# Both pairs of down-projection blocks of a gated conv-FFN by seven products, evicted by ScalarE and summed by accumulating DMAs

## What is computed

```python
def rms_norm(x, g):
    xf = x.astype(jnp.float32)
    return (xf * lax.rsqrt(jnp.mean(xf * xf, axis=-1, keepdims=True) + EPS)) * g

def conv_gated_ffn(x, w_up, conv_w, conv_b, w_down):     # x 256 x 2048, w_up 2048 x 11264
    gu = x @ w_up
    gate, up = gu[..., :D_FF], gu[..., D_FF:]            # D_FF = 5632
    gate = causal_depthwise_conv(gate, conv_w, conv_b)   # three taps along the tokens
    return (jax.nn.silu(gate) * up) @ w_down             # w_down 5632 x 2048

h = h + conv_gated_ffn(rms_norm(h, norm_ffn_g[i]), w_up[i], conv_w[i], conv_b[i], w_down[i])
```

## Time and profile before

| | |
|---|---|
| median of 3 runs | 2156.36 us (2156.32 to 2156.4) |
| profiled execution | 2156.12 us, span of its instructions 2154.3 us |
| PE busy | 2141.7 us (99%), 11526 matmuls |
| PE weight load busy | 1859.3 us (86%) |
| DVE busy | 1707.6 us (79%) |
| ACT busy | 1125.1 us (52%) |
| POOL busy | 50.4 us (2%) |
| DMA | 406.75 MB, mean 189 GB/s, the load queue 55.0% of 16 engines |

### The profile page before, as it was taken

The page is one execution under the profiler, slowest core; times in us unless marked ns, Lnnn a source line. Parts: engine busy times, 40 slices in busy tenths (PEclk is TensorE's granted clock), DMA queues, the critical chain, the costliest instruction groups (busy, mean ns, idle before and its releaser), DMA issues.

```text
span 2154.3 us, 32719 instructions
## 1 busy us (share of the span) xinstructions
PE 2141.7 (99%) x11526; PEld 1859.3 (86%) x11526; DVE 1707.6 (79%) x2192; ACT 1125.1 (52%) x1422; POOL 50.4 (2%) x114
## 2 busy tenths in 40 slices
PE   9999999999999999999999999999999999999998
PEld 8898888888888888888898988888888888888886
DVE  5797569888889888897557875788888889888964
ACT  6556445554555544555554664445544545544554
POOL 2000000000000000000000000000000000000011
PEclk9999999999999999999999999999999999999999
DMA  8645555546555546555556455555556555556562
GB/s 269 213 139 174 178 200 188 182 158 233 205 204 178 182 166 234 197 192 195 173 183 182 138 176 176 201 203 176 186 177 234 195 197 176 183 185 234 176 216 97
DMA packets 233323, 406.75 MB, mean 189 GB/s; under 512 B 14828, under 2 KB 50268, under 8 KB 233096
## 3 DMA queue, kind: packets, MB, share of 16 engines
q1 hardware_dynamic: 231976, 402.72, 55.0%
q0 software_dynamic: 512, 1.76, 0.2%
q10 hardware_dynamic: 736, 1.07, 0.1%
HBM read 403.42 MB, written 2.10 MB: 188 GB/s over the span
## 4 chain that ended last, share of the span: by engine, by line
PE 97%; ACT 1%; DVE 1%; issue 1%; POOL 0%; POOLq 0%; DVEq 0%; ACTq 0%
PE acc L2082 16%; PE tps L2082 16%; PE acc L1901 12%; PE acc L1903 12%; PE acc L1902 12%; PE tps L2092 9%; PE acc L2092 9%; PE tps L1902 3%; PE tps L1903 3%; PE tps L1901 3%; PE acc L1988 1%; PE tps L1958 1%; ACT sq_h L773 0%; DVE h L1536 0%; DVE xb_lo L1193 0%
## 5 line engine op out<-in xcount | busy, mean ns | idle before, releaser
L996 ACT ACTIVATE w_hi<-raw 128x1024 fp32r<-128x1024 f32 x540 | 559.2, 1058 | 536.3 <-PE acc L2092 116.6
L1566 DVE TENSOR_TENSOR w_lo<-raw,w_hi 128x1024 fp32r<-128x1024 f32 x540 | 650.2, 1225 | 161.5 <-ACT w_hi L996 149.8
L1181 DVE TENSOR_TENSOR w_lo<-raw,w_hi 128x1024 fp32r<-128x1024 f32 (+1 forms) x288 | 342.0, 1211 | 143.2 <-ACT w_hi L722 137.6
L722 ACT ACTIVATE w_hi<-raw 128x1024 fp32r<-128x1024 f32 (+2 forms) x287 | 290.2, 1044 | 179.5 <-PE acc L1903 126.3
L2082 PE MATMUL acc<-xa,w_hi 128*128 128x512 f32 x1536 | 366.0, 391 | 0.0
L2082 PE MATMUL tps<-xa,w_hi 128*128 128x512 f32 x1536 | 361.2, 390 | 0.0
L2082 PEld LDWEIGHTS tps<-xa,w_hi 128*128 128x128 f32 x1536 | 285.3, 188 | 57.2
L2082 PEld LDWEIGHTS acc<-xa,w_hi 128*128 128x128 f32 x1536 | 283.7, 188 | 56.2 <-DVE h L1521 0.4
L1902 PE MATMUL acc<-w_hi,xb_lo 128*128 128x512 f32 x640 | 249.0, 389 | 0.0
L1901 PE MATMUL acc<-w_hi,xb_hi 128*128 128x512 f32 x560 | 220.5, 394 | 0.4 <-ACT pw L1072 0.4
L1903 PE MATMUL acc<-w_lo,xb_hi 128*128 128x512 f32 x560 | 218.1, 389 | 0.0
(11 more groups left out here) (262 smaller groups left out, 2651.1 us busy)
## 6 DMA issues: line engine op xcount, KB each, us to landing
raw<-in_w_up SPq DMA_DIRECT2D x176, 1024.0 KB, 5.0
raw<-in_w_down SPq DMA_DIRECT2D x88, 1024.0 KB, 5.0
raw<-in_w_out SPq DMA_DIRECT2D x32, 1024.0 KB, 5.0
raw<-in_w_ple_gate SPq DMA_DIRECT2D x32, 1024.0 KB, 5.1
raw<-in_w_in SPq DMA_DIRECT2D x21, 1024.0 KB, 5.4
raw<-in_w_ukv SPq DMA_DIRECT2D x8, 1024.0 KB, 5.5
raw<-in_w_in SPq DMA_DIRECT2D x8, 864.0 KB, 4.8
raw<-in_w_uq SPq DMA_DIRECT2D x6, 1024.0 KB, 5.7
```

The source lines that it names most:

```text
L722: copy(w_hi[:, half_of(m), 0:n], raw[:, c % RAW_SLOTS, at:at + n], ACT.Copy).then_inc(hi_done, 1)
L996: copy(w_hi[:, half_of(m), :], raw[:, c % RAW_SLOTS, half * HALF:(half + 1) * HALF], ACT.Copy).then_inc(hi_done, 1)
L1181: dve.tensor_tensor(w_lo[:, half_of(m), 0:n], raw[:, c % RAW_SLOTS, at:at + n], w_hi[:, half_of(m), 0:n].bitcast(F32), ALU.subtract).then_ ...
L1566: dve.tensor_tensor(w_lo[:, half_of(m), :], raw[:, slot, half * HALF:(half + 1) * HALF], w_hi[:, half_of(m), :].bitcast(F32), ALU.subtract ...
```

## The change

The down product of unit u - 1 is now seven products for both pairs of blocks (0 and 1: `second` = 0; 2 and 3: `second` = 1). A unit has 30 halves in two phases of 15: the gate's 8 halves with the first pair's seven products between them, then the up's 8 halves with the second pair's seven. Within a phase the x halves are at places 0, 1, 2, 3, 5, 8, 11, 14 (`X_AT`), the products B11, B21, B22, T1, T3, T2, T4 at 4, 6, 7, 9, 10, 12, 13 (`FORM_AT`). The loop turns over one unit, and the last unit stands behind it with its second phase "apart" (x halves first, then products). The products of phase A use `tps`, those of phase B `acc`. up_sum and gated of a unit move to the start of the next one.

DVE adds no product any more. ACT evicts each into a buffer `stage` in SBUF, scaled by token where it goes to `h` (`take`, 14 a unit), and POOL adds it with a DMA that accumulates from `stage` into `h` or a sum (`products_added`, 14 a unit, 256 KB each). TensorE waits on `staged` for banks; ACT waits on `stage_free`, which POOL raises when a phase's seven DMAs have landed. There are now two sets of four sums (`corner_b` is new), s_hi and s_lo have their own place, the last unit's low part goes from POOL to DVE, and ACT waits for `stage_free` before the squares of the ple part.

The core of the diff (declarations, the semaphores' count functions, and renamed arguments are left out):

```diff
+        X_AT = (0, 1, 2, 3, 5, 8, 11, 14)
+        FORM_AT = (4, 6, 7, 9, 10, 12, 13)
...
+
+            return max(n for n in range(UNIT_HALVES) if raw_half(n, apart)[0] == c)
+
...
+                def load_at(l, v, n, apart, pieces):
                     slot = (c + n) % RAW_SLOTS
-                    first = M_UNIT + i * UNIT_HALVES + 2 * RAW_SLOTS
                     if n < RAW_SLOTS:
-                        freed = max(LAST_LO[n] + 1 - UNIT_HALVES, 2 * (n + 1) - 2 * RAW_SLOTS)
+                        freed = max(last_lo(n + 2 * RAW_SLOTS, False) + 1 - UNIT_HALVES, 2 * (n + 1) - 2 * RAW_SLOTS)
                     else:
-                        freed = 2 * (n - RAW_SLOTS) + 2
...
+                def load_unit(l, u, v, apart):
+                    for second in range(2):
+                        last = apart and second == 1
+                        for k, n in enumerate(X_CHUNK_APART if last else X_MIXED):
+                            if n == (4 if last else 5):
+                                break
+                            load_at(l, v, PHASE_CHUNKS * second + n, apart,
+                                    (rows(w_up, l, 4 * k, 4, u * BLK + D_FF * second, BLK), CHUNK, BLK))
+                        for k, n in enumerate(Q_APART if last else Q_MIXED):
+                            load_at(l, v, PHASE_CHUNKS * second + n, apart,
+                                    (rows(w_down, l, v * 4, 4, (2 * second + k) * BLK, BLK), CHUNK, BLK))
+                        if not last:
+                            load_at(l, v, PHASE_CHUNKS * second + X_MIXED[3], apart,
...
+                def products_added(v, second):
+                    p1, p7, p6, p5 = sums[second]
+                    j = 2 * second
+                    for k, dst in ((B11, p1), (B21, h[:, 0, j * BLK:(j + 1) * BLK]),
+                                   (B22, h[:, 0, (j + 1) * BLK:(j + 2) * BLK]), (T1, p5), (T3, p7), (T2, p6),
+                                   (T4, h[:, 1, j * BLK:(j + 1) * BLK])):
+                        pool.wait_ge(staged, taken(l, v, second, k + 1))
+                        pool.sem_inc(stage_seen, 1)
+                        pool.dma_start(dst, stage[:, k, :], accum_op=ALU.add).then_inc(added, 16)
+                    pool.wait_ge(added, 16 * 7 * phases(l, v, second))
+                    pool.sem_inc(stage_free, 1)
...
+                    def take(second, k, bank, scale=None):
+                        n = PHASE * second + (FORM_APART if apart and second else FORM_AT)[k]
+                        halves_used(act, l, M_UNIT + n, v)
+                        if k == B11:
+                            act.wait_ge(stage_free, phases(l, v, second))
+                        if scale is not None:
+                            copy(stage[:, k, :], bank, ACT.Copy, scale=rstd["ffn"][:, scale:scale + 1]).then_inc(staged, 1)
+                            return
+                        copy(stage[:, k, :], bank, ACT.Copy).then_inc(staged, 1)
 
...
                     go(0, 2)
-                    halves_used(act, l, m0 - 1, w)
+                    up_low(u - 1, lambda: halves_used(act, l, M_UNIT - 1, v))
+                    go(2, 3)
                     act.wait_ge(g_done, UNITS * l + u)
...
-                    copy(s_hi.rearrange("p c k s -> p (c k s)"), up_f[:, :, :].rearrange("p a s -> p (a s)"),
+                    go(3, 5)
+                    act.wait_ge(s_step, 4 * (UNITS - 1) * l + 4 * v + 4)
+                    copy(s_hi[:, :, :, :].rearrange("p c k s -> p (c k s)"), up_f[:, :, :].rearrange("p a s -> p (a s)"),
                          ACT.Copy).then_inc(s_split_hi, 1)
...
+                    take(0, B11, tps[:, 0, :])
                     go(7, 9)
-                    for k in range(2):
...
-                first_unit(l)
-                with act.Fori(0, LOOPS) as w:
-                    for i in range(TURN_UNITS):
-                        unit(l, w, i)
-
-                act.wait_ge(g_done, UNITS * l + UNITS)
-                copy(xa[0][:, 0:4, :], conv[:, :, :], ACT.Copy).then_inc(g_hi, 1)
+                    take(0, B21, tps[:, 1, :], 0)
+                    go(9, 10)
+                    take(0, B22, tps[:, 2, :], 0)
+                    go(10, 12)
+                    take(0, T1, tps[:, 3, :])
+                    go(12, 13)
+                    take(0, T3, tps[:, 0, :])
+                    go(13, 15)
+                    take(0, T2, tps[:, 1, :])
+                    take(0, T4, tps[:, 2, :], 1)
+                    go(15, 17)
+                    gate_low(lambda: halves_used(act, l, M_UNIT + PHASE - 1, v))
+                    go(17, 21)
+                    silu(u)
+                    if not apart:
+                        go(21, 22)
+                        take(1, B11, acc[0][:, 0, :])
+                        go(22, 24)
+                        take(1, B21, acc[0][:, 1, :], 0)
+                        go(24, 25)
+                        take(1, B22, acc[1][:, 0, :], 0)
+                        go(25, 27)
+                        take(1, T1, acc[1][:, 1, :])
+                        go(27, 28)
+                        take(1, T3, acc[0][:, 0, :])
+                        go(28, 30)
+                        take(1, T2, acc[0][:, 1, :])
+                        take(1, T4, acc[1][:, 0, :], 1)
+                        return
+                    go(21, 25)
+                    up_low(u, lambda: halves_used(act, l, M_UNIT + PHASE + 7, v))
+                    go(25, 26)
+                    take(1, B11, acc[0][:, 0, :])
+                    go(26, 27)
+                    take(1, B21, acc[0][:, 1, :], 0)
+                    act.wait_ge(g_done, UNITS * l + UNITS)
+                    copy(xa[0][:, 0:4, :], conv[:, :, :], ACT.Copy).then_inc(g_hi, 1)
+                    go(27, 28)
...
+                            split_u(v, n + AHEAD, apart)
 
                     go(0, 2)
+                    up_sum(u - 1)
+                    gated(u - 1)
+                    go(2, 3)
+                    s_sums(v, 0)
+                    s_sums(v, 1)
                     dve.wait_ge(g_hi, UNITS * l + u)
                     lo(gt[1][:, :, :], conv[:, :, :], gt[0][:, :, :]).then_inc(g_lo, 1)
...
+                    s_sums(v, 2)
+                    s_sums(v, 3)
+                    go(3, 4)
+                    t_sum(v, 0, apart, 1)
                     go(4, 5)
-                    s_sums(w, i, 2)
+                    t_sum(v, 0, apart, 2)
+                    dve.wait_ge(s_split_hi, (UNITS - 1) * l + u)
+                    dve.tensor_tensor(s_lo[:, :, :, :].rearrange("p c k s -> p (c k s)"),
+                                      up_f[:, :, :].rearrange("p a s -> p (a s)"),
+                                      s_hi[:, :, :, :].rearrange("p c k s -> p (c k s)").bitcast(F32),
+                                      ALU.subtract).then_inc(s_split_lo, 1)
                     go(5, 6)
...
+                    t_sum(v, 0, apart, 3)
+                    go(6, 7)
+                    t_sum(v, 0, apart, 4)
+                    go(7, 10)
+                    go(10, 12)
+                    go(12, 17)
                     gate_sum(u, 0)
                     gate_sum(u, 1)
...
                     gate_normed()
-                    go(10, 11)
+                    go(17, 18)
                     tap_2(u)
...
+                    go(18, 19)
+                    if not apart:
+                        t_sum(v, 1, apart, 1)
+                        tap_1(u)
+                        go(19, 20)
+                        t_sum(v, 1, apart, 2)
+                        tap_0(u)
+                        go(20, 21)
+                        t_sum(v, 1, apart, 3)
+                        go(21, 22)
+                        t_sum(v, 1, apart, 4)
+                        go(22, 25)
+                        go(25, 27)
+                        go(27, 30)
+                        return
...
+                    corners_summed(0, 0)
+                    corners_summed(0, 1)
+                    go(20, 21)
+                    t_sum(v, 1, apart, 1)
+                    corners_summed(0, 2)
+                    corners_summed(0, 3)
+                    go(21, 22)
+                    t_sum(v, 1, apart, 2)
+                    t_sum(v, 1, apart, 3)
+                    go(22, 23)
+                    t_sum(v, 1, apart, 4)
+                    go(23, 25)
                     up_sum(u)
...
                     gated(u)
...
+                    go(25, 27)
+                    dve.wait_ge(g_hi, UNITS * l + UNITS)
+                    lo(xa[1][:, 0:4, :], conv[:, :, :], xa[0][:, 0:4, :]).then_inc(g_lo, 1)
...
+                    ins.then_inc(w_used, 1)
...
+                    def gate_acc(f, first):
+                        if first:
+                            pe.wait_ge(staged, taken(l, v, 0, 0))
+                        if first and f % 2 == 0:
+                            free_acc(l, b0 + f // 2, v)
+                        return acc[f // 2][:, f % 2, :]
+
```

(21 more changed lines are left out.)

420 lines of the change are left out of this document (219 added, 201 removed).

## The result

The changed kernel takes 2451.84 us (median of 4 runs, 2449.32 to 2453.54) against 2156.34 us: ratio 1.137, interval 1.135 to 1.1389. The direction of the forecast was right and its size was not: 2189 was said, at most 2240, and the loss is 295 us instead of 33.

The account below looks back on a forecast made before the run. TensorE was taken to be full and to bound the kernel: -27.2 us of matmuls, +55 of waits on delayed loads, +4 at layer ends gave +32, 2189 us. The range for 8 in 10 was 2140 to 2240 us.

Parts of the forecast that it names:

- What is removed from TensorE: Down blocks in the loop: six matmuls fewer, 1.36 us a unit, 27.2 us in 20 units; new unit 63.49 us.
- The sums of DVE and ACT: Busy time in a loop unit: DVE 57 and ACT 44 of 63.5 us, neither the bound by sums.
- The chain of phase A and phase B: DVE to T4's split, load, two splits, evictions: slack 0.55 us in A, TensorE waits 1.2 in B, 21.6 us.
- the walk: The prediction's step-by-step timing of each loop phase from its start, and of the layer's end, giving TensorE's waits.
- x = 0: Delay of each of two critical loads by accumulating DMAs: none if they miss each other; 0.96 us was taken.
- rival (2): Loop: accumulating DMAs miss the loads, -27.2 + 21.6 + 4 = -1.6, 2155 us; chance 0.15, the same.
- What the accumulating DMAs do to those loads: Loop: one DMA delays each of two loads by 0.96 us; A waits 0.4, B 2.6, together 55 us.
- Rival (4): Loop: two accumulating DMAs of two passes hit each load, A waits 2.0, B 4.2; 2250 us, chance 0.20.
- Rival (5): Loop: POOL's descriptor writing holds DVE up, 0.77 us for each of 14 issues; 2219 us at least, chance 0.05.
- Rival (1): Loop: loads don't end last and nothing stalls; 2133 us, or 2143 with 0.5 us a unit of waiting; chance 0.22.
- A page against the row: 256 KB DMA: page gives 2.6 us, row 4.8, same sum; the page's shared 16 engines speak against the change.
- The end of each layer: Layer end: last low part and kept sums on DVE cost 2 us a layer, 4 in all, bounds 0 and 8.

Follow-up runs that it names:

- f_thin_order: Changed kernel with low parts, sums and gate eviction ahead of late splits, two taps and silu later, accumulating DMAs moving 32 of 512 words; 2145.86 us.
- a_thin: Changed kernel with each accumulating DMA moving 32 of 512 words, issues and waits kept, most of every sum left out; 2250.16 us, ratio 1.0436.
- a_pool: Changed kernel with POOL adding each staged product itself by a tensor_tensor in SBUF instead of by a DMA; 2301.74 us, ratio 1.0672.
- g_both: Changed kernel, complete: queues reordered, five DMAs a phase held back except a layer's last, ScalarE's first block awaiting two DMAs, corner sums later; 2149.37 us.
- d_acc: Kernel before, with 14 accumulating DMAs of 256 KB a unit from POOL, of zeros into an unread buffer; 2182.05 us, ratio 1.0119.

## Why the prediction was wrong, by its own steps

**What is removed from TensorE** held nearly: 63.49 us a unit was said, and the kernels without stops have 63.65. That is 1.2 us a unit instead of 1.36, 24 us in all.

**The sums of DVE and ACT** held: 57 and 44 us of 63.5 were said. In f_thin_order DVE is busy 463.34 and ACT 348.88 of 520 us, that is 56.7 and 42.7 a unit:

```profile
420.00:940.00 520.00, 519.77 (x2774) 449.45 (x2773) 463.34 (x505) 348.88 (x406) 94.88 (x112) 1.00 0.62 199
```

Two slips in its arithmetic change nothing: eight evictions of 0.60 and six of 0.68 us are 8.9, not 8.6, and the terms of its sum give 2188, not 2189.

**The chain of phase A and phase B** is the step that failed first. It was the right chain, and its last link was in place: TensorE does wait for T4 at the unit's start, 1.2 us without other data by the walk and 2.0 in a_thin. But the walk let each phase begin as if the loads were there ("ACT's split 4 ends about 0.9"; "splits 19 and 20 end at 0.9 and 1.9"). That split needs the third load of the train that T4's split of the phase before sets off. It comes 2.2 to 2.6 us late in a_thin and 6.41 in the stop shown above; DVE, with 22 us of work in series behind it, hands the delay on to its own T4 split, and so to the next train. The loop closes on itself, with no idle place in it, and the walk had cut it open at its start. The walk gave each load the 5.0 us of a lone one too, and the `w_down` loads of a train land after 9.2. The price can be read without the bytes: by the walk with x = 0, rival (2), the kernel takes 2155 us, and a_thin, with a sixteenth of the data, takes 2250. The prediction had named the sign itself (a wait of TensorE for `g_lo` would mean that its clock of DVE's order is wrong), and the kernel after has 16 such waits, 37.8 us.

**What the accumulating DMAs do to those loads** was mis-sized in two factors. One DMA, x = 0.96 us, was taken for each of two loads. A DMA holds the engines 1.48 us, above the bound of two passes (1.28). And it isn't one: the `w_down` loads of the train land 14.3 - 9.2 = 5.1 us later than with thin DMAs, as much as three to four of them take, and four were issued within 6 us around it. In the loop the bytes cost 9.3 us a unit, where 2 x 0.96 were taken.

**The rivals.** Rival (4), two DMAs of two passes on each load, named the right direction ("a load that is delayed meets the next one too"), and at 2250 us had still the open walk under it. Rival (5) had the wrong mechanism: POOL's 280 issues leave DVE's operations at 1219 ns. Its engine pair does interfere when POOL computes (a_pool). Rival (1) is what g_both comes near to, from the same diff in another order.

**A page against the row.** The sentence of the Trainium skill's DMA: Bandwidth & Descriptors (section "Issuing engines are not separate DMA queues") that all issuers share the same 16 engines was the one that spoke against the change. The rows agree (share 1.06 to 1.10 while loads and accumulating DMAs run together), and d_acc shows its limit: shared engines cost nothing in the loop where the loads have slack.

**The end of each layer.** 2 us a layer was said, with 4 as the upper bound; E is 11.6 us longer. The walk priced DVE's extra sums and left out that ScalarE now waits there for POOL's last DMA to land. Freed of that wait, E is 2.5 to 4.6 us a layer longer than before's, about the upper bound.

**The clock** had no term. Behind four stops of 3.07 to 3.50 us in the kernel after, TensorE's clock is at half for 3.4 to 6.8 us, in part still within the stop; of a_thin's shorter ones, one of 2.08 us has 3.4 us at half behind it and one of 2.02 us none. Work done at half the clock takes twice its time, so a long stop costs an estimated 1.7 to 3 us beyond itself, half of the busy part of these stretches. It follows from the stops and isn't a cause of its own.

**Where the gain went in g_both.** The matmuls give back 12 us a layer. F falls by 8.2 (first layer) and 7.2 (second), and E gives back 4.0 and 4.6. That leaves 6.8 of 24. What F lacks of 12 is for the most part POOL's pause: the two units at it take 65.88 and 64.23 us instead of 63.65 in the first layer, 66.84 and 64.30 in the second, together 2.8 and 3.8 us. One us a layer remains, beside the last unit. Whether the pause or that rest can go wasn't tried. Also open: of a_thin's 5.2 us a unit above the floor, idle time of TensorE in its window is 17.1 of 340 us, some 3.5 a unit, and the granted clock of 0.99 another 0.7; the records put no name to the rest.

## What to carry to other kernels

When a change moves work into a fixed order between loads, walk the order once around, from a load to the release that asks for the same slot again, and start the second turn where the first ended; a walk that starts with all loads landed can't find a closed chain. Price a load by how many are asked for together, not by a lone one, and keep other DMAs out of the stretch in which a train of them lands: holding seven DMAs back, without one byte less, took 174 us off this kernel. And look up at every new wait which part of a resource it needs: ScalarE needed two of seven places free and waited for all.

## What the runs showed of the hardware

- An accumulating DMA of 256 KB from SBUF to SBUF takes 1.48 us of all 16 DMA engines' time, a copy of the same size 0.65 us (by their queue's share of the span).
- While such DMAs and loads run together, the engines are full (share 1.06 to 1.10) at some 260 GB/s in the stretch shown; a load alone reached 410.
- Of a train of four loads of 1 MB issued in under 4 us, the last two land after 9.2 us in the median (a_thin), where loads of before landed after 5.0; with some four accumulating DMAs among them, after 14.3.
- A POOL addition of SBUF operands slows VectorE's beside it (a split 1218 to 1411 ns in the mean), POOL's issuing of DMAs doesn't.
- Behind four stops of TensorE of 3.07 to 3.50 us its granted clock was 0.50 (1.2 GHz) for 3.4 to 6.8 us; of two stops of 2.0 and 2.1 us in a_thin one had such a stretch behind it.
- POOL, issuing accumulating DMAs, stood still for 8.4, 4.0 and 3.0 us in each layer of g_both, with nothing in the profile that ended it; in the seven kernels that hold DMAs back the longest of them in the first 625 us is 8.2 to 9.5 us.
